# A hybrid attention and mixture-of-experts layer: spare products in the routing gap, and a new order of small VectorE work, casts and row transposes

## What is computed

```python
t = rmsnorm(x, norm2_g)                                   # 1024 x 1024
g_prob = softmax(t @ rg_w + rg_b)                         # 4 groups, the best one is taken
e_sel  = (t @ re_w + re_b) restricted to that group       # 8 experts, the best two are taken
gates  = g_top_p * softmax weights of the two, normalised
for e in range(32):                                       # D_EXPERT = 256
    y = (silu(t @ e_gate[e]) * (t @ e_up[e])) @ e_down[e]
    out += combine[:, e:e+1] * y
x = rmsnorm(x + out, final_g)
```

## Time and profile before

| | |
|---|---|
| median of 3 runs | 846.71 us (846.6 to 847.55) |
| the profiled execution | 846.11 us, span 844.3 us |
| TensorE busy | 757.2 us, 90% of the span |
| VectorE, ScalarE, GpSimd busy | 505.8, 435.2, 284.7 us |
| DMA | 160.39 MB, 190 GB/s over the span |
| mean granted clock | 0.967 |

### The profile page before, as it was taken

One profiled execution on the slowest core, in us unless ns is written; L12 is line 12 of the kernel. 1 busy time (PEld: TensorE's weight loads), 2 busy tenths in 40 slices (PEclk: granted clock), 3 DMA queues, 4 the chain that ended last, 5 costly groups with the idle time before them and its releaser, 6 DMA issues.

```text
span 844.3 us, 10463 instructions
## 1 busy us (share of the span) xinstructions
PE 757.2 (90%) x3900; PEld 544.0 (64%) x3900; DVE 505.8 (60%) x772; ACT 435.2 (52%) x635; POOL 284.7 (34%) x240
## 2 busy tenths in 40 slices
PE   3899999999996888899899569999999999999993
PEld 2788888876664555488788546666656666655651
DVE  4651000017767888541347678888888887778737
ACT  6311112115565887710121358888777777777614
POOL 2513355615645777060010121322232332222112
PEclk9999999999998999999899569999999999999998
DMA  8371111100010000332371946999999999999369
GB/s 285 85 193 50 50 42 40 44 1 1 2 51 1 0 1 1 123 102 102 147 262 64 349 152 248 373 379 381 368 370 371 369 377 374 374 370 356 116 247 376
DMA packets 54947, 160.39 MB, mean 190 GB/s; under 512 B 9344, under 2 KB 24160, under 8 KB 46576
## 3 DMA queue, kind: packets, MB, share of 16 engines
q1 hardware_dynamic: 48352, 142.26, 46.5%
q0 software_dynamic: 6400, 16.92, 6.0%
q10 hardware_dynamic: 144, 0.52, 0.2%
HBM read 145.01 MB, written 18.87 MB: 194 GB/s over the span
## 4 chain that ended last, share of the span: by engine, by line
PE 59%; DMA 19%; DVE 9%; ACT 6%; issue 3%; SPq 2%; DVEq 0%; POOL 0%; POOLq 0%; ACTq 0%
DMA wgu<-in_expert_w_up 13%; PE ps L640 6%; PE ps L641 6%; PE ps L642 6%; PE ps L867 4%; PE ps L872 4%; PE ps L875 4%; PE ps L763 3%; PE ps L765 3%; PE ps L764 3%; PE ps L705 2%; DVE wgulo L1598 2%; PE ps L680 2%; PE ps L721 2%; PE ps L894 2%
## 5 line engine op out<-in xcount | busy, mean ns | idle before, releaser
L1598 DVE TENSOR_TENSOR wgulo<-wgu,unit 128x2048 fp32r<-128x2048 f32 x64 | 144.1, 2289 | 46.0 <-ACT unit L1157 46.0
L1157 ACT CAST unit<-wgu 128x2048 fp32r<-128x2048 f32 x64 | 120.4, 1910 | 34.1 <-DMA wgu<-in_expert_w_up 26.3
L1842 POOL DMA_INDIRECT expert_rows<-ysb,idx x32 | 51.4, 1607 | 169.4 <-ACT ysb L1204 160.0
L640 PE MATMUL ps<-hThi,whi 128*128 128x512 f32 x224 | 88.8, 396 | 4.2 <-DVE hTlo L1265 4.2
L642 PE MATMUL ps<-hThi,wlo 128*128 128x512 f32 x224 | 88.2, 394 | 0.0
L641 PE MATMUL ps<-hTlo,whi 128*128 128x512 f32 x224 | 88.1, 393 | 0.0
L1604 DVE TENSOR_TENSOR wdlo<-wd,unit 128x2048 fp32r<-128x2048 f32 x32 | 73.4, 2293 | 6.1 <-ACT unit L1166 6.1
L867 PE MATMUL ps<-unit,xThi 128*80 128x512 f32 x256 | 72.7, 406 | 0.0
L872 PE MATMUL ps<-unit,xTlo 128*80 128x512 f32 x256 | 69.8, 394 | 0.0
L875 PE MATMUL ps<-wgulo,xThi 128*80 128x512 f32 x256 | 69.1, 391 | 0.0
L1797 POOL TENSOR_SCALAR pswa<-pswa,esum 128x384 f32<-128x384 f32 (+1 forms) x48 | 55.6, 1167 | 31.7 <-DVE esum L1353 31.3
(11 more groups left out here) (200 smaller groups left out, 1496.3 us busy)
## 6 DMA issues: line engine op xcount, KB each, us to landing
wgu<-in_expert_w_gate SPq DMA_DIRECT2D x32, 1024.0 KB
wgu<-in_expert_w_up SPq DMA_DIRECT2D x32, 1024.0 KB
wd<-in_expert_w_down SPq DMA_DIRECT2D x32, 1024.0 KB, 16.5
y<-expert_rows SPq DMA_DIRECT2D x16, 512.0 KB, 9.4
wraw<-in_w_in SPq DMA_DIRECT2D x14, 512.0 KB, 3.8
xin<-in_x SPq DMA_DIRECT2D x8, 512.0 KB, 5.6
xres<-in_x SPq DMA_DIRECT2D x16, 256.0 KB, 3.2
out<-fo SPq DMA_DIRECT2D x8, 512.0 KB, 8.8
```

Source lines behind the costliest of these rows:

```text
L640: nc.tensor.matmul(bank, whi[i % 2][:, k, :], hThi[:, k, cols], start=(k == 0), stop=False)
L1157: nc.scalar.copy(weight_unit(e, a)[:], raw_half(wgu, e, a)).then_inc(ahi_done, 1)
L1598: nc.vector.tensor_tensor(raw_half(wgulo, e, a), raw_half(wgu, e, a), weight_unit(e, a)[:].bitcast(F32), ALU.subtract).then_inc(alo_done, 1)
```

## The change

- TensorE: three batches of products whose result nobody reads (`fill`: 13, 4 and 20, each 128 x 128 with the identity) are put between the token lists and the first expert. The first `rank` moves ahead of the second half of an `out_proj`. In the loop over experts `x_rows(e+1)` stands ahead of `h_rows(e-1)`, and `x_rows(1)` between the two halves of `gate_up(0)`.
- ScalarE: one SiLU of an unused 128 x 8 tile stands ahead of the casts. The first half of expert 1's weights is cast ahead of `x_high(0)`. In the loop `x_high` stands ahead of `h_high`, and the second half of the next expert's weights is cast behind `silu(e)`.
- VectorE: in the loop over token tiles `normalise2(t)` stands ahead of `x1T_take(t+1)`, and the routing of the first half is cut into pieces that are spread over three tiles. The expert numbers `ek` are made in two pieces, `experts_of(0)` ahead of `idx` and `experts_of(1)` behind it. `gates_and_counts` stands ahead of the first weight split. In the loop `gated(e)` stands between the two halves of `half_low(e+1)`.
- GpSimd: the registers of a gather are set ahead of its waits.

```diff
+FILL_CHOICE, FILL_ROWS, FILL_GATHER = 13, 4, 20
...
@@ TensorE, rank(g)
                 if g == 0:
                     pe.wait_ge(logit_done, TT - 3)
+                else:
+                    pe.wait_ge(x1T_b, TT)
...
+            def fill(n):
+                for _ in range(n):
+                    nc.tensor.matmul(ps[:, 3, 0:P], ident[:], ones[:], start=True, stop=True)
...
                 x1_transposes(t, 0)
+                if t == TT - 2:
+                    rank(0)
                 out_proj(1, t, range(4, KT))
                 if 1 <= t < TT - 1:
                     logits(t - 1)
-                if t == TT - 2:
-                    rank(0)
...
             lists(0)
+            pe.wait_ge(x1_done, 2 * TT)
+            fill(FILL_CHOICE)
             rank(1)
+            fill(FILL_ROWS)
             lists(1)
             pe.wait_ge(all_summed, 1)
             nc.tensor.matmul(ps[:, 6, 0:N_EXP], ones[:], rs[:, 19, :], start=True, stop=True).then_inc(count_mm, 1)
+            fill(FILL_GATHER)
...
@@ gate_up(e)
                 for a in range(2):
+                    if e == 0 and a == 1:
+                        x_rows(1)
...
             for e in range(N_EXP):
+                if 1 <= e < N_EXP - 1:
+                    x_rows(e + 1)
                 if e >= 1:
                     h_rows(e - 1)
-                if e + 1 < N_EXP:
-                    x_rows(e + 1)
                 gate_up(e)
...
@@ ScalarE
+            nc.scalar.activation(junk[:], stat[:, 3, :], ACT.Silu).then_inc(junk_done, 1)
             half_high(0, 1)
             act.wait_ge(gates_made, 1)
+            half_high(1, 0)
             x_high(0)
             for e in range(N_EXP):
+                if e + 1 < N_EXP:
+                    x_high(e + 1)
                 if e >= 1:
                     h_high(e - 1)
-                if e + 1 < N_EXP:
-                    x_high(e + 1)
+                if e == 0:
+                    half_high(1, 1)
+                elif e + 1 < N_EXP:
                     half_high(e + 1, 0)
-                    half_high(e + 1, 1)
...
                 silu(e)
                 if e < N_EXP - 1:
+                    if e >= 1:
+                        half_high(e + 1, 1)
                     down_high(e)
...
@@ VectorE, the loop over token tiles
                 if t == TG + 1:
-                    choose_pair(0)
+                    choose_second(0)
+                    tile_hots(0)
                 if t == TG + 2:
-                    tile_hots(0)
+                    rows_of(0)
+                normalise2(t)
+                x1T_take(t + 1, 0)
+                if t == TG:
+                    choose_first(0)
+                if t == TG + 1:
                     step(v.tensor_reduce(rs[:, 18, :], rt2[:, 0:TG, :].rearrange("p t e -> p e t"), AX_X, ALU.add))
-                    rows_of(0)
-                x1T_take(t + 1, 0)
-                normalise2(t)
...
             v.tensor_reduce(rs[:, 19, :], rt2[:].rearrange("p t e -> p e t"), AX_X, ALU.add).then_inc(all_summed, 1)
+            experts_of(0)
...
@@ VectorE, the experts
+            experts_of(1)
+            gates_and_counts()
             half_low(0, 0)
-            gates_and_counts()
+            x_low(0)
             half_low(0, 1)
-            x_low(0)
+            half_low(1, 0)
             for e in range(N_EXP):
+                if e + 1 < N_EXP:
+                    x_low(e + 1)
                 if e >= 1:
                     h_low(e - 1)
-                if e + 1 < N_EXP:
-                    x_low(e + 1)
+                if 1 <= e < N_EXP - 1:
                     half_low(e + 1, 0)
-                    half_low(e + 1, 1)
                 if e == N_EXP - 1:
                     down_low(e)
                 gated(e)
                 if e < N_EXP - 1:
+                    half_low(e + 1, 1)
                     down_low(e)
...
@@ GpSimd
             def gather(e):
+                limit = bound(bound_x, S - 1)
+                if e == 0:
+                    for i in range(2):
+                        pool.wait_ge(h2_stored[i], 16 * (TT // 2))
+                    pool.wait_ge(idx_done, 1)
                 if e >= 2:
                     pool.wait_ge(etr_done, e - 1)
```

28 lines of the change are left out of this document (16 added, 12 removed).

## The result

The changed kernel takes 837.48 us (median of 4 runs, 836.41 to 839.55) against 847.1 us (4 runs, 846.6 to 847.55): a ratio of 0.990, 95% interval 0.987 to 0.993. The profiled execution took 836.75 us with a span of 834.9. It is faster by 1%, and the time lies inside the range, 1.6 us above the forecast. A later set of nine runs on another chip gives a smaller gain, 6.0 us instead of 9.6 (see "The changed kernel once more").

A forecast was written before the change was run, and what follows sets the result against it. The prediction took full DMA engines to bound the kernel, their stream starting at the end of `down(0)`. Gains of 8.3 us at the start and 2.5 at the end, 10.8, gave 835.9 us against the median; range 830.5 to 842.

The forecast's parts named there:

- What bounds the kernel: Full DMA engines bound the weight stream; the end of `down(0)`, 512.4 us, starts it, and each us earlier moves the stage.
- Residual and first batch: Last token tile and `fill(13)`: residual 1.0 us earlier, batch 3.0 to 5.6 us; together -1.6 to +2.3, 0 taken.
- `rank(1)` 1.1 and lists 1.0: Second rank and lists at full instead of half clock: gains of 1.1 and 1.0 us, 0 if the clock stays down.
- Registers 0.7: Gather's register instructions set ahead of its wait on GpSimd: 0.7 us saved (0.5 to 0.85).
- Contention -0.3 (0 to -1): First gather, starting about 480, meets weights of experts 2 and 3 on the DMA engines: 0.3 us lost.
- Experts 0 and 1: From `x_rows(0)` to the end of `down(0)`, new order at full clock: gain 6.7 us, 5.8 taken for a possible half-clock stretch.
- the rule of the page: Transposes do not count as TensorE activity as products do; the gap before `gate_up(0)` counts as idle, sum 0.9 us smaller.
- The end, 2.5 of 2.9: After the last weight waits, `wgu` landing to `gate_up` takes 5.0 instead of 7.9 us: gain 2.9, 2.5 taken.
- A clock that does not come back: Rival: spare batches stay at half clock, 5.6 and 8.6 us long; 844.4 us in full, 13 in 100 for parts.
- A loop bound by its latency: Rival: transfers in the expert loop are latency, not bandwidth; 2.9 us saved per turn, 823 us, 7 in 100.
- An order too slow on VectorE: Rival: waits in the new expert-loop chain make an expert take 10.6 us and starve the stream; 851 us, 5 in 100.
- Something that cancels: Rival: rows land late because their store or a wait at the gather comes last; 845 to 848 us, 5 in 100.

The follow-up runs named there:

- The changed kernel once more: The changed kernel repeated without any edit on another chip, nine runs: 839.92 us, ratio 0.992 to the kernel before.
- both edits: Changed kernel with gate/up weights issued ahead of the previous expert's down weights, expert 3's weights behind both first gathers, and 24 spare products in the last batch: 833.86 us.
- the old loop: Changed kernel with the earlier order of the loop over experts restored from expert 2 on: 840.76 us, ratio 0.995.
- the old tiles: Changed kernel with the earlier token-tile order restored: `x1T_take` ahead of `normalise2`, first-half routing in two pieces, `rank(0)` behind the projection: 840.7 us, ratio 0.995.
- batches-alone run: Kernel before with only the three batches of spare products (13, 4, 20) added: 846.15 us, ratio 1.000.
- order-alone run: Changed kernel without its spare products (0, 0, 0): 840.13 us, ratio 0.993.
- the one with 32 products: Changed kernel with gate/up weights issued ahead of the previous expert's down weights, and 32 instead of 20 spare products in the last batch: 832.33 us.
- the swap: Changed kernel with SyncE issuing an expert's `wgu` ahead of the previous expert's `wd`, from expert 5 on: 833.44 us, ratio 0.985.
- the extra products: Changed kernel with two spare 512-column products in each `gate_up` from expert 1 on: 837.39 us, ratio 0.989.

## Why the prediction was right, point by point

The stretches that the change touches gave nearly what was forecast: 2.5 and 5.1 us at the start and 2.9 at the end, 10.5 of 10.8. Around them lie +2.4, -2.3 and -1.3 us that the sum did not have, and terms inside it cancel, as told below. So the mechanism is right, and part of the closeness of the number is luck; on the second chip the measured gain is 6.0 us.

*What bounds the kernel.* Right. D moved, the full stretch moved with it and kept its length to 1%, and 12 us of extra work in it cost nothing. The stage got no shorter than 259.9 us in any run, and there the stream starts ahead of D.

*Residual and first batch, 0.0 taken, -1.6 to +2.3.* `rank(1)` starts 9.4 us behind the last projection instead of 11.4: +2.0, near the upper end, because in the profiled execution the clock never fell before the batch (3.12 us for 13 products, 3.0 forecast). The run with both edits shows the other branch that the sum weighed: 5.13 us, 5.6 forecast, and no gain. Of the eleven traced executions with this batch three went that way (5.13, 4.72 and 3.77 us: both edits, the old loop, the old tiles). The likeliest value was too careful; the bounds held.

*`rank(1)` 1.1 and lists 1.0.* 1.05 and 1.04 us.

*Registers 0.7.* This step failed. From the end of the write of `idx` to the gather 0.91 us remain, 1.06 in before: 0.15 us. The issue gap of 0.61 us stands between the wait and the gather with the register instructions gone from it, so they were not what filled it. The 0.7 rested on taking the gap for the register work beside it.

*Contention -0.3 (0 to -1).* Mis-sized and outside its bounds: -1.7. The prediction set the gather's start at 480; it came at 476.6, with the weights of experts 2 and 3 under way until about 482. The earlier the lists, the more of those weights lie ahead of the rows. Holding expert 3 back, with `idx` at the same 14.0 us, cut the gather to 4.2 us, which shows the cause. The 5.06 us of before, which the term started from, are another matter: that gather is issued latest of all, and from 484 to 486 us the DMA share beside it is 0.05 to 0.06. GpSimd's record of it lasts 2.14 us, in the batches-alone run too, and 1.14 in every run with the new order of the experts' start, where VectorE's first weight split no longer stands right behind `idx`. That some 1 us of the 5.06 is this, and no contention on the DMA engines, is my estimate from these records; no run has that one edit alone.

These three errors, +2.0, -0.55 and -1.4, cancel: to the first transposes 2.5 us were forecast, against 2.5 measured. A right sum here says little for its terms.

*Experts 0 and 1, 24.1 to 17.4 us at full clock, 5.8 of 6.7 taken.* The counted order holds: 17.6 or 17.7 us in the three runs in which the clock stayed up all the way and no later gather was waited for. In the changed kernel the stretch takes 19.0, a gain of 5.1, since TensorE waited 3.29 us for the rows and one stretch at the lower clock was paid in full where the prediction took half. By the rule of the page "TensorE: Matmul & The Clock Gate" of the Trainium skill, section "Part 4: PE-mode transpose", the sum would have been 0.9 lower; the measured 5.1 is 0.7 lower. What the runs show is that the long empty wait ahead of the transposes goes with the lower clock: with that wait filled the transposes run in the same place and the clock stays at 1.00. The old loop's run, in which it fell after 0.79 us, keeps the wait from being the whole cause, and no run separates the rule from it.

*The end, 2.5 of 2.9.* 2.9: from the landing to `gate_up` 5.0 us as worked out (7.9 in rows 11), and the old loop gives 2.8 us back.

*What was not foreseen.* The stretch ahead of the last projection is 2.4 us shorter. In before the clock fell at TensorE's wait for the first `x` of the output projection; in the profiled execution of the changed kernel it did not, at nearly the same wait. Stretches of before, then of after, and the transposes there:

```profile
408.00:412.00 4.00, 4.00 (x14) 3.32 (x13) 2.71 (x2) 0.94 (x3) 0.81 (x2) 0.50 0.21 70
```

```profile
407.23 1.97 PE L776 MATMUL ps<-ident,x 128*128 128x128 f32 x8 [3.06 <-DVE x L1398]
```

```profile
408.00:412.00 4.00, 4.00 (x26) 3.49 (x25) 2.24 (x2) 1.22 (x3) 0.81 (x2) 1.00 0.22 70
```

```profile
407.61 1.09 PE L780 MATMUL ps<-ident,x 128*128 128x128 f32 x8 [3.18 <-DVE x L1421]
```

The order-alone run has it fall there too (0.50 from 408 to 412), the one with 32 products not. Over the fourteen traces it fell in eight, wholly or for a part of the stretch, and stayed in six, among these the batches-alone run, whose code is that of before up to there: it goes by execution, not by the change. From these transposes to the end of the last projection it takes 53.8 us in the six and 55.3 to 56.5 in the eight. Against it stand the last loads and the combination, 33.9 us in the one trace of before and 34.5 to 36.1 in nearly all others, and the stage, 264.3 us in that trace and 265.3 to 266.6 in all later ones without the swap. The batches-alone and old-loop runs have the longer stage too, so the new loop is not its cause. The rates times the lengths, 370 GB/s by 264.4 us and 369 by 266.7, differ by 0.6 MB, 1.6 us; which transfers these are, and whether before has them in other executions, stays open.

*The rivals.* A clock that does not come back: in three of eleven executions the first batch ran slow, wholly or in part, but `rank(1)` behind it ran at full clock each time; batches that stay slow were never seen. A loop bound by its latency: refuted by the extra products and by the old loop, whose stage is as long. An order too slow on VectorE: VectorE has 80.80 us in 91.80 while TensorE has no gap. Something that cancels: in part, at the gather.

*The swapped queue* beats both kernels, by 6.5 us under the changed kernel on the same chip. Spare products up to the landing of the rows make its trace shorter still; more runs would be needed to show that in the time.

## What to carry to other kernels

Find the moment from which the transfers are continuous. Until then a us can count once (the batches alone moved D by 2.0 us in their trace and the time by nothing that ten runs show), behind it nothing counts but the last transfer's successors, and the cheapest gain may be to issue the next weights ahead of a wait that they do not depend on. Spare products pay up to the moment at which the real ones can start and cost beyond it: the batch that ended 3.2 us early left 1.5 us that the longer one took, and one that began at half clock ran past that moment and held the transposes up. Before speeding up the road to a gather, look at what is queued on the DMA engines when it would start.

## What the hardware showed that I had not expected

Three things. The clock at one and the same wait of TensorE fell, in part at least, in eight executions and stayed in six, and the length of the wait does not part them: the shortest, 2.93 us, is among the eight and the longest, 3.52 us, among the six. The 0.61 us between GpSimd's wait and its first gather do not belong to the register instructions. And GpSimd's records of the gathers nearly doubled in the full stage, groups by line of before and then of after:

```profile
L1835 POOL DMA_INDIRECT xg<-h_rows,idx x28 | 32.4, 1156 | 59.3 <-PE ps L845 59.3
```

```profile
L1873 POOL DMA_INDIRECT xg<-h_rows,idx x27 | 60.1, 2226 | 31.7 <-PE ps L860 27.4 <-issue 4.3
```

Single ones take up to 5.16 us, when they are issued while VectorE runs its splits back to back:

```profile
493.78 5.16 POOL L1873 DMA_INDIRECT xg<-h_rows,idx  x1 [2.48 <-PE ps L860]
```

```profile
493.63 2.28 DVE L1632 TENSOR_TENSOR wgulo<-wgu,unit 128x2048 fp32r<-128x2048 f32 x1
495.83 2.28 DVE L1638 TENSOR_TENSOR wdlo<-wd,unit 128x2048 fp32r<-128x2048 f32 x1
```

The mean goes with the order of the work: it is 1163 ns in the batches-alone run, 1652 in the old-loop run and 1839 to 2379 in all runs with the new loop. That GpSimd and VectorE share something is my guess from where the records fall; no run here tested that alone. It cost nothing that TensorE's waits show: from D to the end of the experts TensorE waits only for `hx` and, once, 1.2 us for the last `ysb` (view of waits, after):

```profile
PE ps L899 <- DVE hx L1663: 11.5, 14, 2.8
```
